# A transformer pair's first feed-forward stage as one level of Strassen's block product

## The reference

```python
h = rms_norm(x, norm2_g[l])                                          # x: (1, 1024, 1024)
x = x + (jax.nn.silu(h @ w_gate[l]) * (h @ w_up[l])) @ w_down[l]      # D_FF = 2816
```

## Time and profile before

| what | value |
|---|---|
| runs (3) | 2729.75, 2730.13, 2730.36 us; median 2730.13 |
| the profiled execution | 2728.0 us, its span 2726.3 us |
| mean granted clock of TensorE | 0.954 |
| PE busy | 2504.2 us, 92% |
| VectorE busy | 1215.7 us, 45% |
| GpSimd busy | 831.9 us, 31% |
| ScalarE busy | 691.8 us, 25% |
| DMA | 126.42 MB, mean 46 GB/s |

### The profile page before, as it was taken

How to read it: one execution, slowest core, us unless ns; L and a number is a source line. 1 busy time by engine, 2 the same in 40 slices (tenths; PEclk the granted TensorE clock), 3 DMA queues, 4 the chain that set the end, 5 groups by cost and what they waited for, 6 DMA issues and landing times.

```text
span 2726.3 us, 27582 instructions
## 1 busy us (share of the span) xinstructions
PE 2504.2 (92%) x11052; PEld 1960.1 (72%) x11052; DVE 1215.7 (45%) x1223; ACT 691.8 (25%) x938; POOL 831.9 (31%) x390
## 2 busy tenths in 40 slices
PE   8988877999999999998988987795999999999979
PEld 6866645788888888886755554484888888888857
DVE  7788853332222222325555555548222222222465
ACT  4255543210000000003054646513111000110231
POOL 1000001443444344434311210045334333433353
PEclk9989988999999999999988987897999999999989
DMA  3210102111111111112100000110111111111112
GB/s 123 59 34 23 31 16 77 47 39 55 47 47 52 48 46 46 50 43 104 47 16 16 24 8 1 78 54 17 53 47 46 47 53 46 46 50 50 54 31 85
DMA packets 47793, 126.42 MB, mean 46 GB/s; under 512 B 19105, under 2 KB 19105, under 8 KB 45665
## 3 DMA queue, kind: packets, MB, share of 16 engines
q1 hardware_dynamic: 47056, 120.89, 14.7%
q10 hardware_dynamic: 656, 4.41, 0.4%
HBM read 116.68 MB, written 8.79 MB: 46 GB/s over the span
## 4 chain that ended last, share of the span: by engine, by line
PE 75%; issue 10%; DVE 8%; ACT 4%; POOL 2%; DMA 1%; SPq 0%; POOLq 0%; DVEq 0%; ACTq 0%
PE ps L501 66%; PE ps L904 3%; PE ps L836 1%; ACT sb_e L1294 1%; ACT sb_e L1292 1%; POOL branch_out L460 1%; POOL weight_hi L418 1%; DMA weight_raw<-w_out 1%; ACT sb_e L1296 1%; DVE sb_softplus_lo L1859 1%; POOL weight_lo L420 1%; DVE residual L1966 1%; DVE conv_out L1515 1%; PE ps L879 1%; PE ps L613 1%
## 5 line engine op out<-in xcount | busy, mean ns | idle before, releaser
L418 POOL TENSOR_TENSOR weight_hi<-weight_raw,zero_col 128x1024 fp32r<-128x1024 f32 (+1 forms) x174 | 331.6, 1906 | 1800.8 <-PE ps L501 1549.1
L501 PE MATMUL ps<-input_hi,weight_hi 128*128 128x512 f32 x1904 | 607.2, 400 | 59.0 <-DVE input_lo L1473 35.5
L501 PE MATMUL ps<-input_lo,weight_hi 128*128 128x512 f32 x2032 | 638.7, 396 | 19.2 <-DVE gate_lo L1970 17.4
L501 PE MATMUL ps<-input_hi,weight_lo 128*128 128x512 f32 x1904 | 593.1, 393 | 0.0
L501 PEld LDWEIGHTS ps<-input_hi,weight_hi 128*128 128x128 f32 x1904 | 358.0, 191 | 149.2 <-issue 56.0
L501 PEld LDWEIGHTS ps<-input_lo,weight_hi 128*128 128x128 f32 x2032 | 388.6, 192 | 105.2 <-ACT input_lo L1010 14.0
L420 POOL TENSOR_TENSOR weight_lo<-weight_raw,weight_hi 128x1024 fp32r<-128x1024 f32 (+1 forms) x174 | 443.2, 2547 | 13.7
L501 PEld LDWEIGHTS ps<-input_hi,weight_lo 128*128 128x128 f32 x1904 | 362.4, 190 | 77.2
L501 PE MATMUL ps<-hidden_hi,weight_hi 128*128 128x512 f32 x864 | 231.0, 389 | 3.4 <-DVE hidden_lo L1733 3.4
L501 PE MATMUL ps<-hidden_lo,weight_hi 128*128 128x512 f32 x864 | 230.9, 389 | 0.0
L501 PE MATMUL ps<-hidden_hi,weight_lo 128*128 128x512 f32 x864 | 230.9, 389 | 0.0
(11 more groups left out here) (241 smaller groups left out, 2696.1 us busy)
## 6 DMA issues: line engine op xcount, KB each, us to landing
weight_raw<-w_ff SPq DMA_DIRECT2D x40, 512.0 KB, 3.6
weight_raw<-w_mlp SPq DMA_DIRECT2D x32, 512.0 KB, 3.6
weight_raw<-w_mlpd SPq DMA_DIRECT2D x32, 512.0 KB, 3.6
weight_raw<-w_ffd SPq DMA_DIRECT2D x20, 512.0 KB, 3.6
weight_raw<-w_out SPq DMA_DIRECT2D x16, 512.0 KB, 3.6
weight_raw<-w_in SPq DMA_DIRECT2D x16, 512.0 KB, 3.5
weight_raw<-w_qkv SPq DMA_DIRECT2D x12, 512.0 KB, 3.7
weight_raw<-w_glu SPq DMA_DIRECT2D x8, 512.0 KB, 4.1
```

Source lines behind the costliest of these rows:

```text
L418: pool_.tensor_tensor(WH[:, slot, 0:width], raw, ZERO[:].to_broadcast([P, width]), ALU.add).then_inc(s["w_hi"], 1)
L501: last = mm(PS[:, b + 2 * c + h, :], w[:, slot, k * n + P * c:k * n + P * (c + 1)], a[:, k, h * H2:(h + 1) * H2], start=(k == first and st ...
```

## The change

The stage is no longer made of units but of turns. Strassen's product (in Winograd's form) halves both operands and the result in each direction: 7 products of half-size blocks take the place of 8, and sums of blocks are made of the operands ahead of them and of the results behind them. The norm's scale of a token stays outside, so it goes on the results as before.

*Hidden turns*, t = 0 to 21: one for each pair of 128 gate or up channels, with tokens halved (`lower`, `upper`) and k halved (chunks 0 to 3 and 4 to 7). The seven token operands, split high and low, are made once into `FORM` (16 KB each per partition) by VectorE and ScalarE around the last output-projection units and in turn 0. For each turn SP loads two units into `RAWS`, GpSimd makes 4 sums and 7 lows of 512 elements, ScalarE the 7 highs, each in single buffers `WS`. PE's product is 4 k-chunks x 3 = 12 matmuls of 512 tokens. Three PSUM banks take a turn's seven products; ScalarE copies a bank out (`mid`) between two products that share it, VectorE adds later ones.

*Parts*: after each odd turn two hidden chunks are ready; VectorE makes 4 sums and, with ScalarE's 7 highs, 7 lows of them into `STG`, and SP writes them to device memory (`HD`). The residual X is also put aside in device memory (`XD`) at the start of the stage, since its place is needed, and read back for the last sums.

*Output turns*, t = 22 to 33: 6 groups (the first of one part, five of two parts) x 2 halves of the rows, with their operands read back by SP into a ring of ten places; VectorE adds each product to `MM` and at last to X.

All loops of the stage are written out. The diff, cut to the parts that set order and waits:

```diff
+N_PROD = 7
+ROLE = (0, 2, 0, 1, 0, 2, 0)
+FRESH = (True, True, False, True, False, False, False)
+LO_ORDER = (0, 1, 3, 2, 4, 5, 6)
+def reads_to(t):
+    return 4 * min(t, FF_A.n1) + N_PROD * max(0, t - FF_A.n1)
 # SP
+            def turn_load(t):
+                if t >= 2:
+                    sp.wait_ge(s["st_lo"], N_PROD * (t - 1))
...
+            for t in range(2, FF_A.t2 + 2):
+                turn_load(t)
+                if t % 2 == 0 and t >= 4:
+                    parts_out(t // 2 - 2)
 # GpSimd
-            splits(U_OUT + 2, U_TAIL + 2 * TAIL - U_OUT - 2)
-            splits(U_TAIL + 2 * TAIL, 4, TAIL * 256)
-            splits(U_POOL, 2)
+            splits(U_OUT + 2, 6)
+            def turn_split(t):
...
+                lo(0, a11)
+                free(1)      # waits for st_prod of turn t-1's product 1
+                total(1, place(1, 1, WT), a21, a22, ALU.add)
+                free(2)
+                total(2, place(2, 1, WT), place(1, 1, WT), a11, ALU.subtract)
+                total(3, a21, a11, a21, ALU.subtract)
+                lo(1)
+                lo(3, a12)
+                pool.wait_ge(s["st_lo"], low(t, 3))
+                total(4, a12, a12, place(2, 1, WT), ALU.subtract)
+                lo(2)
+                lo(4, a21)
+                lo(5, a12)
+                lo(6, a22)
 # PE
+            def hidden_turn(ff, t):
...
+                for p in range(N_PROD):
+                    pe.wait_ge(s["st_lo"], low(t, p))
+                    if p in (0, 1, 3) and n >= 2:
+                        pe.wait_ge(s["st_read"], reads_to(t - 2) + {0: 4, 1: 3, 3: 1}[p])
+                    elif p in (2, 4, 5):
+                        pe.wait_ge(s["st_mid"], 3 * t + {2: 1, 5: 2, 4: 3}[p])
+                    elif p == 6:
+                        pe.wait_ge(s["st_read"], reads_to(t) + 2)
+                    turn_product(t, p, bank0 + ROLE[p], weights, tokens, 4, True)
+                    if n == 0 and p == 3:
+                        scale_sum(2 * KD)
...
+            pe.wait_ge(s["bank_free"], U_OUT + 8)
 # ScalarE
             for k in range(KD):
+                act.wait_ge(s["bank_free"], U_OUT + k + 1)
+                square(X[:, k, :], (TA, TB)[k % 2][:])
...
+                if k == 6:
+                    for p in range(4):
+                        turn_hi(0, p)
+                if k >= 4:
+                    j = k - 4
+                    act.wait_ge(s["st_op"], OP_SUMS[1, j])
+                    op_hi(FF_A, 1, j, op_raw(FF_A, 1, j))
+                    act.wait_ge(s["st_op"], OP_SUMS[2, j])
+                    op_hi(FF_A, 2, j, X[:, j, lower])
...
+            for t in range(1, FF_A.t2):
+                parts = t // 2 - 1 if t % 2 == 0 else None
+                mid(FF_A, t, 0)
+                turn_hi(t + 1, 0)
+                if parts is not None:
+                    part_hi(parts, 0)
+                    part_hi(parts, 1)
+                mid(FF_A, t, 1)
+                turn_hi(t + 1, 1)      # then part_hi 2, 3
+                mid(FF_A, t, 2)
+                turn_hi(t + 1, 2)      # then part_hi 4, 5, 6
+                turn_hi(t + 1, 3)
+                silu(t, 0)
+                turn_hi(t + 1, 4)
+                silu(t, 1)
+                turn_hi(t + 1, 5)
+                turn_hi(t + 1, 6)
 # VectorE
+            def hidden_terms(ff, t):
+                term(t, 3, GA[:, lower], GA[:, lower], ALU.add)      # bank + SBUF
+                tt(GA[:, lower], GA[:, lower], RS[:, lower], ALU.mult)
+                term(t, 4, h[:, upper], h[:, upper], ALU.add)
+                tt(h[:, upper], h[:, upper], RS[:, upper], ALU.mult)
+                term(t, 5, GA[:, upper], GA[:, upper], ALU.add)
+                tt(GA[:, upper], GA[:, upper], RS[:, upper], ALU.mult)
+                term(t, 6, h[:, lower], RS[:, lower], ALU.mult)
+                tt(h[:, lower], h[:, lower], GA[:, lower], ALU.mult)
+                tt(h[:, upper], h[:, upper], GA[:, upper], ALU.mult)
...
+            for t in range(FF_A.t2):
+                hidden_terms(FF_A, t)
+                if t % 2 and t < FF_A.t2 - 1:
+                    part_sums(t // 2)
+                    for f in range(N_PROD):
+                        part_lo(t // 2, f)
+            for t in range(FF_A.t2, FF_A.end):
+                for p in range(N_PROD):
+                    output_term(FF_A, t, p)
+                    if t == FF_A.t2 + 2:
+                        if p == 0:
+                            part_sums(FF_A.n1 // 2 - 1)
+                        part_lo(FF_A.n1 // 2 - 1, p)
```

More of the change, by code:

```diff
@@ L338, in _, with x_kept @@
+            def x_kept(k):
+                sp.wait_ge(s["bank_free"], U_OUT + k + 1)
+                sp.dma_start(XD[:, k, :], X[:, k, :]).then_inc(s[f"st_x{min(k, 4)}"], 16)
             for j in range(8):
                 load_unit(U_OUT + j, j % 2, w_out[j])
[L340 to L346, removed]
@@ new lines, in _ @@
+            for p in range(N_PROD):
+                parts_in(FF_A, 0, p)
+            for t in range(FF_A.t2, FF_A.end):
+                g, r, _ = FF_A.group(t)
+                if t + 2 < FF_A.end:
+                    turn_load(t + 2)
+                if g + 1 < len(FF_A.groups):
+                    for p in ((0, 1, 2), (3, 4, 5, 6))[r]:
+                        parts_in(FF_A, g + 1, p)
+                if g == 1 and r == 0:
+                    parts_out(FF_A.n1 // 2 - 1)
+                elif g == 1:
+                    for n in range(3):
+                        sp.wait_ge(s[f"st_sp{n}"], 16 * FF_A.n1 // 2)
+                    for k in range(2):
+                        sp.dma_start(X[:, 4 * k:4 * k + 4, :], XD[:, 4 * k:4 * k + 4, :]).then_inc(s["st_back"], 16)
@@ L763, in ff_group, with turn_product @@
                          k_ready=hidden if m == 0 else None)
[L765 to L773, removed]
+            def turn_product(t, p, b, weights, tokens, n, last):
+                for k in range(n):
+                    for step, (w, a) in enumerate(((0, 0), (0, 1), (1, 0))):
+                        ins = mm(PS[:, b, :], weights(p, w, k), tokens(p, a, k),
+                                 start=(FRESH[p] and k == 0 and step == 0), stop=(k == n - 1 and step == 2),
+                                 skip_group_check=True)
+                if last:
+                    ins.then_inc(s["st_prod"], 1)
@@ L774, in _ @@
+            pe.wait_ge(s["bank_free"], U_OUT + 8)
+            for t in range(FF_A.t2):
+                hidden_turn(FF_A, t)
+            for t in range(FF_A.t2, FF_A.end):
+                output_turn(FF_A, t)
+            pe.wait_ge(s["st_read"], reads_to(FF_A.end - 1) + 4)
+            first_two(U_POOL, inputs(KD, KD))
+            pe.wait_ge(s["st_read"], reads_to(FF_A.end))
             scale_sum(3 * KD)
@@ new lines, in _ @@
+            for j in range(4):
+                op_hi(FF_A, 5, j, X[:, 4 + j, upper], g("norm2", 4 + j))
+            turn_hi(1, 1)
+            turn_hi(1, 2)
+            first_guess(bank(6), RS[:], "mean_done", 2, "ln_exp")
+            for j in range(4):
+                act.wait_ge(s["st_op"], OP_SUMS[6, j])
+                op_hi(FF_A, 6, j, op_raw(FF_A, 6, j))
+            turn_hi(1, 3)
+            silu(0, 0)
+            turn_hi(1, 4)
+            silu(0, 1)
+            turn_hi(1, 5)
+            turn_hi(1, 6)
```

447 lines of the change are left out of this document (381 added, 66 removed).

## The result

The changed kernel takes 2734.9 us (median of 12 runs, 2731.8 to 2736.7), the one before 2729.7 (12 runs beside them, 2728.3 to 2733.0): a ratio of 1.0017, interval 1.0009 to 1.0025. It is 5.2 us slower: just under the 0.2% that was to count, but clear of the runs' noise, and not the forecast 10 us faster. A saving of 90 us in matmuls was spent to the last microsecond.

The account below looks back on a forecast made before the run. PE, busy with matmuls, was taken to bound the stage: 628.1 + 23 + 66 + 2.5 + 5 + 2 + 1.5 = 728.1 against 738.1 us, 10.0 faster, so 2720 us; range 2664 to 2752.

Parts of the forecast that it names:

- 2772 matmuls: Whole stage: PE's matmuls fall from 3168 to 2772 at an unchanged 0.2266 us each: 628.1 us, 89.7 less.
- ten waits, product 7: Even hidden turns: PE waits 5.0 us before product 7 for VectorE's second read, ten times: 50 us.
- clock behind them: Behind PE's ten hidden-turn waits: matmuls slowed by lost clock, 1.6 us each by a mean, 16 us in all.
- start, with turn 1's wait: Turns 0 and 1: PE starts 4.8 us late, operands lag, turn 1's third product held 2.5: 23 us with clock.
- into the output turns: Behind turn 21's products: seven adds of 1.22 us out of banks, in turns of 9.52: 2.5 us.
- third output turn: Last part split there: VectorE's second read 3.4 us late, its fourth 0.6; with clock 5 us (0 to 7).
- adds, loads, out: Residual's extra adds, and loads: 2 us; leaving the stage, the second unit's weights split behind product 6: 1.5 us.
- point of no gain: Hidden turns: 7.6 us a pair, wait and clock, would leave no gain, against the 6.6 taken.
- Rival (a): Hidden turns: the part work fits, product 7 waits under 1 us without clock loss; 2655 us, chance 0.13.
- (d): Rival for the hidden turns: full clock loss behind the wait in every pair; chance 0.13, its size not given here.

Follow-up runs that it names:

- PSUM variant: Changed kernel, but part operations of the first ten splits take one operand from an idle PSUM bank, values left out: 2656.8 us, ratio 0.9730.
- the best version: Changed kernel with the first order, edits of start and output turns, and ScalarE's second odd-turn bank copy waiting for part sums only: 2652.6 us, ratio 0.9715.
- the first order: Changed kernel with VectorE's part work in even hidden turns laid between its reads instead of ahead of them: 2668.4 us, ratio 0.9773.
- the second: As the first order, with part low 2 between the third and fourth read and low 4 ahead of the last: 2669.4 us, ratio 0.9779.

## Why the prediction was wrong

From the last projection matmul (535.72) to the mean behind the next stage's first two units (1302.45), less 21.75 us for those units' 96 matmuls, it is 745.0 us, where 728.1 were predicted and 738.1, taken in the same way, were to be beaten. By the prediction's own steps, with every matmul at its price of 0.2266:

| term | predicted | measured |
|---|---|---|
| 2772 matmuls | 628.1 | 628.1 |
| ten waits, product 7 | 50 | 55.7 |
| clock behind them | 16 | 23.4 |
| start, with turn 1's wait | 23 | 26.0 |
| into the output turns | 2.5 | 2.9 |
| third output turn | 5 | 7.1 |
| adds, loads, out | 3.5 | 1.8 |
| sum | 728.1 | 745.0 |

The PSUM variant's 0.2270 a matmul would put 1.1 us more in the first row and as much less in the others.

**What held.** The mechanism, its place and its count: ten waits, all of product 7 in even turns, none in odd ones; part operations at 1.67 to 1.80 beside GpSimd's at 1.59 to 1.73, from the estimate of 1.7 out of the earlier trace rows; PE's share of 0.885 and 0.966 for the 0.88 and 0.98 forecast; the price of a matmul; the third output turn, where VectorE's second read is held up behind part work (PE resumes at the third, right behind it); no wait for a load. Rival (a) needed the part work to fit in the order given, which it does not; but its 2655 is near what the same work takes once the wait is gone: the PSUM variant reaches 2656.8 and the best version 2652.6.

**The step that failed is the clock.** I took 1.6 us a pair, the mean of three losses in the earlier trace rows, of which the one behind the 3.42 us wait was nothing (granted clock 1.00 in the 4.37 us behind it). The two slow restarts lost 1.73 (behind 6.17, at 0.51) and 2.94 (behind 3.20, at 0.50), mean 2.3, and the ten measured ones run from 1.7 to 3.0, mean 2.35. A recurring wait of one length in one loop is not a draw from all waits of a trace. The full loss in every pair is what (d), with 0.13, stands for, and all ten pairs had it; with the wait filled, 168 matmuls take 38.37 to 38.39 us instead of 39.8 to 41.05. What was missed by it (23.4 against 16) is 7.4 of the 16.9 us.

**The wait itself was written out right and then shaved.** The schedule said 21.9 against 16.33, which is 5.57; 5.58 came. I had taken 0.5 off for an overlap of ending and starting operations, and by that 5 to 6 us in all. With both, a pair costs 7.9 us where 6.6 were taken; the prediction's own point of no gain was 7.6. So the sign hung on 0.3 us a pair, and a forecast of faster with 0.62 was too sure of it. (The ten waits' 66 us of the 89.7 saved were three quarters, not two thirds.)

**The start** was 3 us short. PE began 6.76 after the last projection matmul, not 4.8; product 5 at 26.3, not 22.6 (561.98 - 535.72); and turn 0, whose product 7 ran at half clock (0.50 granted in 573.20 to 577.40), closed near 577.4, which is 41.7 where 38.8 stood. The list of VectorE's operations was right and their durations in turn 0 too short; which of the 27 ran longer stays open. **The third output turn** paid 2.6 of clock (0.61 granted in 1096.84 to 1101.20) besides its 4.41. On the way into the output turns the wait is 1.04, and 1.8 more lie in the row of 120 behind it, at a granted clock of 1.00; their cause stays open.

The profiled pair is 6.5 us apart, the medians 5.2: 6.9 in the stage so measured, 2.4 more ahead of it and 2.7 less behind it. The 2.4 need no cause: in the profiles of the eight experiments, with nearly the same code ahead, the last projection matmul ends anywhere from 530.15 to 537.23. For the 2.7 no run was made.

## What to carry to other kernels

When a change trades one engine's work for work of two others that share a resource (here a part operation takes 1.67 to 1.80 us beside one of GpSimd's and 0.68 without), add up the shared resource first (here 22 operations of GpSimd and 21 of VectorE in each 38 us), then write the queues out at the point where the critical engine next needs one of them: the total fitted, and the order did not. Put work that nobody waits for *between* the reads that release the critical engine, never ahead of them; here that alone was worth 66 us. And charge a recurring wait as long as these (5.58 us) with the full slow restart each time (1.7 to 3.0 us here), not with an average over unlike waits.

## What the hardware showed beyond that

The clock loss behind ten equal waits of 5.58 us (the first 5.49) was not one number: the pairs took, in order, 40.63, 39.77, 40.91, 39.88, 40.99, 39.95, 41.05, 39.98 and 40.98 us, so the loss alternates between some 1.85 and 2.9 us. With the waits of 0.75 us of the first order and of 1.0 us of the second, which stand ahead of product 5 of odd turns, the 168 matmuls took 0.3 and 0.5 beyond the plain 38.07, and the granted clock stayed at 1.00 in 620 to 980. Extra matmuls whose result nobody reads paid for themselves where PE's own restart lay on the path (22 us), and brought nothing where another engine's chain did (turn 0: 2662.2 against 2662.4 us).
